# Wide remainder splits and half-tile loads of expert rows in the down stage of a decoder step

## What is computed

```python
    def chunk(hc):
        qry = (hc @ w_query).reshape(-1, PEER_HEADS, 2, PEER_HALF)
        ...
        gate = jax.nn.softmax(top_s, axis=-1).astype(hc.dtype)
        act = jax.nn.gelu(jnp.einsum('cd,chkd->chk', hc, expert_u[idx]))
        return jnp.einsum('chk,chkd->cd', gate * act, expert_v[idx])
```

## Time and profile before

| | us |
|---|---|
| median of 3 runs | 2219.4 |
| lowest, highest | 2213.34, 2234.45 |
| the profiled execution, by its own time | 2225.7 |
| its span in the profile | 2224.0 |
| mean granted TensorE clock in it | 0.993 of full speed |

### The profile page before, as it was taken

How to read it: one execution, slowest core, us unless ns; L and a number is a source line. 1 busy time by engine, 2 the same in 40 slices (tenths; PEclk the granted TensorE clock), 3 DMA queues, 4 the chain that set the end, 5 groups by cost and what they waited for, 6 DMA issues and landing times.

```text
span 2224.0 us, 55792 instructions
## 1 busy us (share of the span) xinstructions
PE 2187.3 (98%) x16578; PEld 2140.6 (96%) x16578; DVE 1663.1 (75%) x3039; ACT 1215.7 (55%) x2217; POOL 691.6 (31%) x516
## 2 busy tenths in 40 slices
PE   9999999999999999999999999999999998999997
PEld 8999899999999999999999999999999998999997
DVE  8777788887766667888885444476788886888887
ACT  6445366667455445555555544455555654655664
POOL 0221100002011000788888888300623233111120
PEclk9999999999999999999999999999999999999999
DMA  7887756666556556887876888698889988899985
GB/s 240 283 294 235 240 188 211 200 214 220 183 184 209 170 168 183 189 180 186 188 179 168 208 186 182 174 336 266 252 275 325 335 298 281 267 291 299 299 282 184
DMA packets 337993, 514.36 MB, mean 231 GB/s; under 512 B 87276, under 2 KB 126564, under 8 KB 337772
## 3 DMA queue, kind: packets, MB, share of 16 engines
q1 hardware_dynamic: 263244, 427.59, 61.2%
q0 software_dynamic: 58016, 71.54, 12.8%
q10 hardware_dynamic: 16640, 14.16, 2.0%
HBM read 487.87 MB, written 25.24 MB: 231 GB/s over the span
## 4 chain that ended last, share of the span: by engine, by line
PE 73%; DMA 2%; DVE 1%; issue 1%; ACT 0%; DVEq 0%; ACTq 0%; SPq 0%
PE ps L2167 17%; PE ps L314 15%; PE ps L317 15%; PE ps L313 15%; PE ps L2171 9%; DMA gat<-expert_v,gidx 1%; DVE lo L301 0%; DMA raw<-expert_v 0%; PE ps L2191 0%; PE ps L1394 0%; DVE gacc L2033 0%; ACT hi L296 0%; DVE x L2148 0%; PE ps L2200 0%; DVE fin_r L374 0%
## 5 line engine op out<-in xcount | busy, mean ns | idle before, releaser
L301 DVE TENSOR_TENSOR lo<-raw,hi 128x512 fp32r<-128x512 f32 x1504 | 1024.8, 694 | 458.5 <-ACT hi L296 432.9
L296 ACT CAST hi<-raw 128x512 fp32r<-128x512 f32 x1504 | 924.6, 620 | 731.8 <-PE ps L317 441.5
L313 PE MATMUL ps<-h_hi,hi 128*128 128x264 f32 (+1 forms) x3200 | 822.3, 286 | 1.4 <-DVE h_lo L950 1.4
L314 PE MATMUL ps<-h_lo,hi 128*128 128x264 f32 (+1 forms) x3200 | 821.0, 286 | 0.0
L313 PEld LDWEIGHTS ps<-h_hi,hi 128*128 128x128 f32 x3200 | 602.5, 188 | 8.4 <-issue 5.7
L314 PEld LDWEIGHTS ps<-h_lo,hi 128*128 128x128 f32 x3200 | 602.8, 188 | 0.0
L317 PE MATMUL ps<-h_hi,lo 128*128 128x264 f32 (+1 forms) x3200 | 523.9, 285 | 6.0 <-DVE lo L301 5.9
L1726 POOL DMA_INDIRECT w_spill<-chosen,widx x256 | 438.5, 1713 | 268.4 <-DVE widx L1949 188.8
L2167 PE MATMUL ps<-whl,hi 128*128 128x432 f32 x2048 | 491.0, 362 | 1.8 <-ACT half_sum L1810 1.2
L317 PEld LDWEIGHTS ps<-h_hi,lo 128*128 128x128 f32 x3200 | 444.7, 188 | 8.1 <-DVE lo L301 8.1
L2167 PEld LDWEIGHTS ps<-whl,hi 128*128 128x128 f32 x2048 | 349.6, 191 | 10.7 <-issue 1.6
(11 more groups left out here) (302 smaller groups left out, 1724.9 us busy)
## 6 DMA issues: line engine op xcount, KB each, us to landing
raw<-u_tiles SPq DMA_DIRECT2D x512, 256.0 KB, 3.1
raw<-expert_v SPq DMA_DIRECT2D x512, 256.0 KB, 5.9
raw<-weights SPq DMA_DIRECT2D x480, 256.0 KB, 3.3
w_spill<-zeros ACTq DMA_DIRECT2D x16, 864.0 KB, 6.1
wld<-w_spill SPq DMA_DIRECT2D x32, 432.0 KB, 4.4
qb<-q_spill POOLq DMA_DIRECT2D x8, 512.0 KB, 6.2
w_spill<-chosen,widx POOLq DMA_INDIRECT x256
u_spill<-ust SPq DMA_DIRECT2D x128, 24.0 KB
```

What stands on the lines that cost most here:

```text
L296: nc.scalar.copy(hi[k % SPLIT][:], raw_quarter(k)).then_inc(hi_done, 1)
L301: nc.vector.tensor_tensor(lo[k % SPLIT][:], raw_quarter(k), hi[k % SPLIT][:].bitcast(F32), ALU.subtract).then_inc(lo_done, 1)
L313: pe.matmul(out, a, rhs[0][:, first + j, 0:n], start=start and j == 0, stop=False)
L314: pe.matmul(out, a, rhs[1][:, first + j, 0:n], start=False, stop=False)
```

## The change

In the down stage alone:
- **DVE** makes `lo` for a half tile in one instruction of 128 x 1024 elements, where it made it in two of 128 x 512. It has two buffers of that width (the same 4 quarters as before). It waits for `hi` of both quarters and until PE is done with the half tile two before. In step c it splits half tile c+1.
- **ACT** still makes `hi` by quarters, but into eight buffers: the four of before and four more (`hi_more`) in the space of slots 1 and 2 of `wld`. It splits the quarters 2c+5 and 2c+6 in step c (FAR = 5) and waits for `mm_done` of the quarter eight before (four before for the first ones).
- **SP** loads a half tile in one transfer of 512 KB, with rows of 4 KB (`load_whole`), where it issued two of 256 KB with rows of 2 KB. It waits until `hi` and `lo` of *both* quarters of the half tile four before have been made. Only the very first half tile is still loaded by quarters.
- The last four chunks of the weight matrix go to a buffer and a semaphore of their own (`wlast`, `w_in[3]`), and the wait before the first of them is gone. `gacc` moves a little.
- In `halves` the order in a step stays: split, `w_part`, `between`. PE's order does not change; it reads `hi` from eight buffers.

The core of the diff:

```diff
-    hi = [place(f"hi{s}", at["raw"] + 2048 * s, [P, QT, P], F32R) for s in range(SPLIT)]
-    lo = [place(f"lo{s}", at["hi3"] + 2048 * s, [P, QT, P], F32R) for s in range(SPLIT)]
+    hi_all = place("hi", at["raw"], [P, SPLIT * QT, P], F32R)
+    lo_all = place("lo", at["hi"], [P, SPLIT * QT, P], F32R)
...
+    more = at["W"] + 16 * TD
+    gacc = place("gacc", more + 8192, [P, len(GROUPS), HALF * P])
...
+    wlast = place("wlast", at["gacc"], [P, 4, TD])
+    hi_more = place("hi_more", more, [P, SPLIT * QT, P], F32R)
+    hi8 = hi + [hi_more[:, QT * s:QT * s + QT] for s in range(SPLIT)]
+    hi_pair = [(hi_all if s < 2 else hi_more)[:, HALF * (s % 2):HALF * (s % 2) + HALF] for s in range(4)]
+    lo_pair = [lo_all[:, HALF * s:HALF * s + HALF] for s in range(2)]
...
+        def load_whole(c, s, src):
+            sp.wait_ge(hi_done, 2 * c + 2)
+            sp.wait_ge(lo_done, 2 * c + 2)
+            sp.dma_start(raw[:, s].rearrange("p a b -> p (a b)"), src).then_inc(raw_in[s][0], 16)
...
         for s in range(RAW):
-            load_half(sp, C0 + s, s, expert_v[0, s])
+            if s == 0:
+                load_half(sp, C0, 0, expert_v[0, 0])
+            else:
+                load_whole(C0 + s, s, expert_v[0, s])
...
-        sp.wait_ge(w_mul, UP_CHUNKS + 1)
-        cells_in(UP_CHUNKS, 1)
+        cells_in(UP_CHUNKS, 3)
...
-                load_half(sp, C0 + NK + 4 * i + s, s, expert_v[1, 4 * i + s])
+                load_whole(C0 + NK + 4 * i + s, s, expert_v[1, 4 * i + s])
...
+        def split_far(q0, k, free=SPLIT):
+            act.wait_ge(raw_in[k // 2 % RAW][0], 2 * q0 + 16 * (k // (2 * RAW)) + 16)
+            act.wait_ge(mm_done, q0 + k + 1 - free)
+            nc.scalar.copy(hi8[k % (2 * SPLIT)][:], raw_quarter(k)).then_inc(hi_done, 1)
...
+        def split(c, k):
+            for r in range(2):
+                if not (isinstance(c, int) and 2 * c + FAR + r >= 4 * NK):
+                    split_far(2 * C0 + 2 * (c - k), 2 * k + FAR + r)
+        for k in range(AHEAD, FAR):
+            split_far(2 * C0, k, 0 if k < SPLIT else SPLIT)
+        halves(act, split, w_part, between, after_pass)
...
-        for k in range(8):
+        for k in range(7):
             split_lo(dve, 8 * (PAIR_U - 1), AHEAD + k)
...
+        def split(c, k):
+            if isinstance(c, int) and c + 1 >= 2 * NK:
+                return
+            q0, k = 2 * C0 + 2 * (c - k), k + 1
+            dve.wait_ge(hi_done, q0 + 2 * k + 2 * RAW + 2)
+            dve.wait_ge(mm_done, q0 + 2 * k + 2)
+            nc.vector.tensor_tensor(lo_pair[k % 2][:], raw[:, k % RAW], hi_pair[k % 4][:].bitcast(F32),
+                                    ALU.subtract).then_inc(lo_done, 2)
+        halves(dve, split, w_part, between, after_pass)
...
-            a, b = hi[(2 * k + r) % SPLIT], lo[(2 * k + r) % SPLIT]
+            a, b = hi8[(2 * k + r) % (2 * SPLIT)], lo[(2 * k + r) % SPLIT]
```

More of the change, by code:

```diff
@@ L92, in program @@
     raw = place("raw", 0, [P, RAW, HALF, P])
-    hi = [place(f"hi{s}", at["raw"] + 2048 * s, [P, QT, P], F32R) for s in range(SPLIT)]
-    lo = [place(f"lo{s}", at["hi3"] + 2048 * s, [P, QT, P], F32R) for s in range(SPLIT)]
-    ident = place("ident", at["lo3"], [P, P])
+    hi_all = place("hi", at["raw"], [P, SPLIT * QT, P], F32R)
+    lo_all = place("lo", at["hi"], [P, SPLIT * QT, P], F32R)
+    hi = [hi_all[:, QT * s:QT * s + QT] for s in range(SPLIT)]
+    lo = [lo_all[:, QT * s:QT * s + QT] for s in range(SPLIT)]
+    ident = place("ident", at["lo"], [P, P])
     ones = place("ones", at["ident"], [P, P])
@@ L202, in program @@
     wld = place("wld", at["W"], [P, 3, 4, TD])
-    gacc = place("gacc", at["wld"], [P, len(GROUPS), HALF * P])
+    more = at["W"] + 16 * TD
+    assert more + 8192 >= at["wld"]
+    gacc = place("gacc", more + 8192, [P, len(GROUPS), HALF * P])
     gat2 = place("gat2", at["gacc"], [P, HALF * P])
@@ L249, in program @@
     gat.append(gat2)
+    wlast = place("wlast", at["gacc"], [P, 4, TD])
+    assert at["wlast"] <= at["gat2"]
+    hi_more = place("hi_more", more, [P, SPLIT * QT, P], F32R)
+    hi8 = hi + [hi_more[:, QT * s:QT * s + QT] for s in range(SPLIT)]
+    hi_pair = [(hi_all if s < 2 else hi_more)[:, HALF * (s % 2):HALF * (s % 2) + HALF] for s in range(4)]
+    lo_pair = [lo_all[:, HALF * s:HALF * s + HALF] for s in range(2)]
     ps = ctx.enter_context(nc.psum_tensor("ps", [P, 8, 512], F32))
@@ L1532, in program @@
     route, route_seen = sem("route"), sem("route_seen")
-    u_out, w_in, w_mul = [sem("u_out0"), sem("u_out1")], [sem(f"w_in{h}") for h in range(3)], sem("w_mul")
+    u_out, w_in, w_mul = [sem("u_out0"), sem("u_out1")], [sem(f"w_in{h}") for h in range(4)], sem("w_mul")
     soft, soft_act, widx_made = sem("soft"), sem("soft_act"), sem("widx_made")
@@ L1560, in program @@
     FIRST = 4
+    FAR = 5
     LATE_ADDS = [(0, 2, 4, 6), (0, 2, 4, 6), (0, 2, 4, 6), (0, 2, 3, 4)]
@@ L1582, in gather_rows, with halves, half @@
                                      bass.IndirectOffsetOnAxis(ap=index, axis=0)).then_inc(gat_in[row_slot(n)], 16)
-    def halves(eng, w_part, split, between, after_pass):
-        def half(p, i, k, last=2):
+    def halves(eng, split, w_part, between, after_pass):
+        def half(p, i, k):
             c = NK * p + 8 * i + k
-            for r in range(last):
-                split(eng, C0 * 2 + 2 * (c - k), 2 * k + AHEAD + r)
-            if k % 2 == 0 and last == 2:
+            split(c, k)
+            if k % 2 == 0 and not (isinstance(c, int) and c + 2 >= 2 * NK):
                 w_part(c + 2, p, i, k + 2)
@@ L1609, in halves @@
                 for k in range(8):
[L1610 to L1613, removed]
+                    half(p, i, k)
             after_pass(p)
@@ L1626, in cells_in @@
         def cells_in(m, h):
-            sp.dma_start(wld[:, h], w_dram[bass.ds(4 * m, 4)].rearrange("n p t -> p n t")).then_inc(w_in[h], 16)
+            sp.dma_start(wld[:, h] if h < 3 else wlast[:], w_dram[bass.ds(4 * m, 4)].rearrange("n p t -> p n t")).then_inc(w_in[h], 16)
         def u_tiles_in(first, last):
@@ L1687, in stream @@
                 for s in range(RAW):
-                    load_half(sp, C0 + 4 * i + s, s, expert_v[0, 4 * i + s])
-        load_half(sp, C0 + RAW, 0, expert_v[0, RAW])
+                    load_whole(C0 + 4 * i + s, s, expert_v[0, 4 * i + s])
+        load_whole(C0 + RAW, 0, expert_v[0, RAW])
         spill(PAIR_U - 1, 1)
         for s in range(1, RAW):
-            load_half(sp, C0 + RAW + s, s, expert_v[0, RAW + s])
+            load_whole(C0 + RAW + s, s, expert_v[0, RAW + s])
         sp.wait_ge(w_mul, UP_CHUNKS + 4)
-        cells_in(UP_CHUNKS + 1, 1)
+        cells_in(UP_CHUNKS + 1, 3)
         stream(2, 3)
@@ L1701, in experts_sync @@
                     for s in range(RAW):
-                        load_half(sp, C0 + 8 * i + 4 * h + 4 + s, s, expert_v[0, 8 * i + 4 * h + 4 + s])
+                        load_whole(C0 + 8 * i + 4 * h + 4 + s, s, expert_v[0, 8 * i + 4 * h + 4 + s])
                         if first == 1 and h == 1 and s == 0:
                             sp.wait_ge(w_mul, UP_CHUNKS + i + 4)
-                            cells_in(UP_CHUNKS + i + 1, 1)
+                            cells_in(UP_CHUNKS + i + 1, 3)
                 sp.dma_start(x2[:, bass.ds(i, 1)], x2_dram[:, bass.ds(i, 1)]).then_inc(x2_in, 16)
@@ L1822, in between @@
                 scaled(k)
-        halves(act, w_part, split_hi, between, after_pass)
+        def split(c, k):
[5 more added lines that the diff above has]
+        halves(act, split, w_part, between, after_pass)
         nc.scalar.activation(gw[:, 0:2], eps[:], ACT.Sqrt)
@@ L2020, in times_up @@
             wv = W[:, bass.ds(4 * m, 4), :]
-            nc.vector.tensor_tensor(wv, wv, wld[:, h], ALU.mult).then_inc(w_mul, 1)
+            nc.vector.tensor_tensor(wv, wv, wld[:, h] if h < 3 else wlast[:], ALU.mult).then_inc(w_mul, 1)
         def w_part(c, p, i, k):
@@ L2053, in between @@
                     dve.wait_ge(tile_free[b], PAIR_U + 1)
-                times_up(i + UP_CHUNKS, 1, i + UP_CHUNKS // 3)
+                times_up(i + UP_CHUNKS, 3, i)
             if p == 0 and static:
@@ L2142, in experts_vector @@
         w_part(0, 0, 0, 0)
-        halves(dve, w_part, split_lo, between, after_pass)
+        def split(c, k):
[7 more added lines that the diff above has]
+        halves(dve, split, w_part, between, after_pass)
         dve_rstd(dve, LIVE, fin_r[:, 0], fin_r[:, 1], fin_r[:, 2], 4, D, 0, bank(0))
```

## The result

| | before | after |
|---|---|---|
| median, us (6 runs each) | 2222.3 | 2371.3 |
| lowest, highest | 2213.3, 2234.5 | 2369.2, 2374.5 |
| ratio after / before, 95% interval | | 1.067 [1.064, 1.070] |
| span of the profiled execution | 2224.0 | 2368.4 |

The forecast was 2215 with a range from 2209 to 2238. The time is far above it, and it is steady: no run of the changed kernel is near any run of before.

What follows compares the result with a forecast made beforehand. PE was taken to bound the kernel; 2225.7 (profiled execution) - 11.5 (pass 0's self-feeding gather stall not started, or short) + 0.8 (late gathers or loads) = 2215.0 us, range 2209 to 2238.

Steps and rivals of the forecast that it cites:

- What bounds the kernel now: Down stage: PE bounds it at 2.45 us per half tile, except a gather stall of 11.5 us ending pass 0.
- the stall that feeds itself: End of pass 0: with two gather buffers one late gather makes the next late until the pass ends; 11.5 us.
- the short one at the turn of the passes: Between the passes: a short stall that every run has, put at a us or three.
- Wide `lo`: DVE, down stage: the 1024-wide split takes about 1.21 us, between 1.07 and 1.28; worth nothing by itself.
- ACT eight buffers ahead: ACT, down stage: its 224.8 us of waits for PE go and it follows the transfers; no time on PE's path.
- L + 2.7: Loop of one raw slot: landing time L plus 2.7 us, within 9.8 us for four half tiles; L may be 7.1.
- One transfer of 512 KB: Down-stage loads: whole half tiles land after 7.0 us in pass 0 and 6.5 in pass 1, just inside 7.1.
- The wait for the weight chunks, SP's issues: SP: waited 4.2 us at most for the chunks, PE did not; half as many loads issued; worth nothing.
- The first rival: Raw slot becomes the bound if L is over 7.1; 32 us at L = 7.6 everywhere, 2246 us; chance 0.14.
- Less work for the DMA engines: DMA, down stage: 4 KB rows cost less, both queues' share falls from 95% to about 81%; no gain by itself.
- the 22%: DMA saving from 4 KB rows: a half tile costs each engine 1.36 us and not 1.75.
- The gathers as rival: Queues taking turns by row slow gathers to 8.0 us, 8.8 at most, against 8.5; about 2230 us; chance 0.12.

Runs made afterwards that it cites:

- e9: Kernel before with a third gather buffer in pass 0 and its steps 32 to 95 written out; 2251.9 us against 2256.6 before, ratio 0.9974.
- e12: e9 with ACT's `whl` cast ahead of its step's splits; 2251.6 us against 2260.0 for the kernel before, ratio 0.9966.
- e5: Changed kernel with FAR = 4 and ACT's `whl` cast ahead of its step's splits; 2231.4 us against 2220.5 for the kernel before, ratio 1.0054.
- e1: Changed kernel with ACT's `whl` cast ahead of the two `hi` splits of its step; 2272.1 us against 2218.8 for the kernel before, ratio 1.023.
- e2: Changed kernel with FAR = 4 instead of 5; 2295.2 us (one run) against 2218.8 for the kernel before.
- e3: Changed kernel with each half tile loaded as two 256 KB transfers, ACT waiting for each quarter's own; 2320.1 us (one run) against 2218.8 for the kernel before.
- e7: e5 with each half tile loaded as two 256 KB transfers issued together; 2222.0 us against 2220.5 for the kernel before, ratio 1.0010.
- e4: Kernel before with 512 KB loads in the down stage, nothing else; 2250.2 us against 2218.8 for the kernel before, ratio 1.014.
- e11: e4 with ACT's `whl` cast ahead of its step's splits; 2288.7 us against 2256.6 for the kernel before, ratio 1.0139.
- e8: Kernel before with ACT's `whl` cast ahead of its step's splits, nothing else; 2220.5 us against 2220.5 for the kernel before, ratio 0.9999.

## Why the prediction was wrong, step by step

- *What bounds the kernel now*: right that PE does, and that the loss at the end of pass 0 is one of two gather buffers (e9, e12). But the stall that feeds itself is not the usual case, the short one at the turn of the passes is. Removing both is worth 0.3% as a ratio, 7 us, where the one execution I read had 11.5. And I booked it as a gain of the change, which does nothing about it: e5's DVE waits 24.7 us for gathers, before it was 17.8.
- *Wide `lo`*: right. The 1024-wide split takes 1.22 us (forecast 1.21). The lower bound of 1.07 was a slip: by the same slope the fixed part of a split is 689 - 512 x 1.03 = 0.16 us, and two splits less one fixed part are again about 1.21:

```profile
L2176 DVE TENSOR_TENSOR lo<-raw,hi_more 128x1024 fp32r<-128x1024 f32 x128 | 152.6, 1219 | 19.3 <-PE ps L2206 19.0
```

- *ACT eight buffers ahead*: **the step that failed.** I wrote "ACT follows the transfers" and "No time on PE's path". I looked at what ACT no longer waits for, and not at what stands behind its new, earlier wait in its own order: the `whl` cast, for which DVE waits with everything else. The loop of the slot, L + 2.7, held only the work on one half tile; it left out that engines in order tie half tiles together. Measured it is L + 5.65: the cast, DVE's `whl`, the add and the `lo` of the half tile before lie in it too. Mending ACT's order takes back 99 us (e1), 76 (e2, one run) or, with both edits, 140 of the 149 (e5). That is the cost of the order with whole loads; with shorter ones it is less, as e3 shows.
- *One transfer of 512 KB*: the size of L was nearly right, 7.4 us in pass 0 (forecast 7.0) and 6.4 in pass 1 (6.5), and not the 10.0 that L + 2.7 would need for 12.7 us in four half tiles. With the order mended, whole loads cost 9 us (e5 against e7), and 31 in the kernel before (e4), where the loop is L + 4.0.
- *The wait for the weight chunks, SP's issues*: no effect seen.
- *The first rival* named the sign, the chain "PE for `lo`, `hi` for `raw`" and a size of 32 us; its cause (L over 7.1) is at most a small part: L = 7.4 makes L + 2.7 = 10.1 in place of 9.8, 0.3 of the 3.0 us that each turn of pass 0 grew by. The range ended 133 us below the result, because no rival put more work into the loop.
- *Less work for the DMA engines*: wrong. Pass 0, 1700 to 1795, after, against the earlier trace rows:

```profile
q1 hardware_dynamic: 4683, 15.88, 54.3%
q0 software_dynamic: 2284, 7.66, 20.3%
...
raw<-expert_v SPq DMA_DIRECT2D x30, 512.0 KB
```

The load queue took 0.543 x 16 x 95 = 825 us for 15.9 MB, 52 us for a MB; before it was 0.683 x 1520 / 20.9 = 50. The rows of 4 KB are no cheaper for each byte; the 22% did not come. (By its own terms the share should also have been 80% and not 81.) It did fall, from 94.8 to 74.6%, but only because the pace did: four half tiles took 12.8 us and not 9.8, and 74.6 x 12.8 / 9.8 is 97.
- *The gathers as rival*: the direction was right, the reason mostly another. They landed after 8.4 us in the middle (7.5 before) in the same stretch, though the engines had less to do:

```profile
DMA to landing us min/median/max: 7.2/8.4/9.1
```

Over half of the 0.9 us is POOL's own issue of the gather, before and after, 1700 to 1795:

```profile
L1581 POOL DMA_INDIRECT gat<-expert_v,gidx x20: 1020/1142/1145, 1699.0 to 1791.9; - x20
L1592 POOL DMA_INDIRECT gat<-expert_v,gidx x15: 1674/1676/1684, 1699.1 to 1789.5; - x15
```

Its median in this stretch is 1.67 to 1.68 us in every run with the wide splits, e3 and e7 with their 256 KB loads too, and 1.14 to 1.15 in every run without, e4 and e11 with their 512 KB loads too. I had costed the wide split for DVE alone. What is left may be the size of the rows: in e7, with loads in rows of 2 KB and a busier DMA, gathers land after 7.7 us from 1640 to 1880 (7.2 in e8, with the narrow splits), and in e5 after 8.0. The page "DMA: Bandwidth & Descriptors" of the Trainium skill, section "Queues, rings and completion order", says that a DMA engine changes between queues a packet at a time. These 0.3 us, where I had worked out 0.5, go that way; one execution of each is no proof.

## What to carry to other kernels

When an engine is allowed to run further ahead, write down its whole instruction order for one step and mark which load each instruction waits for; everything behind such a wait inherits it, also small work for nearby tiles. Work for near use (here the `whl` cast) goes ahead of work for far use. The loop of a slot is all that stands between a landing and the next load into that slot, in the order of every engine on the way; add it up so, and not along one tile. A larger transfer waits for the last of its parts, so what stands between the parts joins the loop (e4). And a gain read from one execution is one of the change only if the change touches its cause.

## What the runs showed of the hardware

Rows of 4 KB loaded by SP cost the DMA engines about 215 ns each (825 us for 30 x 128 rows, some small parts of `x2` among them), gathered rows of 4 KB in the same stretch 0.203 x 1520 / 1920 = 161 ns. Packet by packet in that trace the median is 159 ns for both; the load's mean is higher because 13% of its packets took over 250 ns, of the gathers' 2%. The loads' rows lie 1 MB apart in DRAM, the gathered ones anywhere. Whether this distance is the cause was not tried.

POOL's issue of a gather ended 0.8 us after the end of the split that DVE was in: in the trace of before the split (0.69 us) ends at 1704.02 and the issue at 1704.82, in that of the changed kernel the split (1.22) ends at 1706.74 and the issue at 1707.55. The issue took 1.14 us in the one and 1.68 in the other, and the 0.53 us more are the difference of the two splits. That POOL cannot begin its part while such a split runs is the reading that fits; no run has tested it alone.
